# Expert up matrices in two transfers: the last three quarters go into the ring slot of the turn ahead

## What is computed

```python
def hier_moe(x, w_group, w_expert, w_gate, w_up, w_down):
    ...
    for e in range(N_EXPERTS):                                  # 32
        hid = jax.nn.silu(xf @ w_gate[e]) * (xf @ w_up[e])      # 1024 -> 512
        out = out + combine[:, e:e + 1] * (hid @ w_down[e])     # 512 -> 1024
```

## Time and profile before

| | us |
|---|---|
| median of three runs | 1307.29 |
| lowest and highest | 1305.0, 1307.72 |
| the profiled execution's own time | 1307.29 |
| its span, first to last instruction | 1305.5 |
| TensorE busy | 1045.1 (80%) |
| bytes read from HBM | 472.08 MB |

### The profile page before, as it was taken

The page is one execution under the profiler, slowest core; times in us unless marked ns, Lnnn a source line. Parts: engine busy times, 40 slices in busy tenths (PEclk is TensorE's granted clock), DMA queues, the critical chain, the costliest instruction groups (busy, mean ns, idle before and its releaser), DMA issues.

```text
span 1305.5 us, 26625 instructions
## 1 busy us (share of the span) xinstructions
PE 1045.1 (80%) x11057; PEld 641.9 (49%) x11057; DVE 483.5 (37%) x965; ACT 176.1 (13%) x413; POOL 108.7 (8%) x233
## 2 busy tenths in 40 slices
PE   9999989666766676679999999999675676756778
PEld 7885555333433333344688884555333333333333
DVE  2987534111111111136685888524121111211127
ACT  2343211000000000011111110211010000000011
POOL 0010111000010000000110110011000000000000
PEclk9999899888888888889999999998888888888889
DMA  9866999999999999999454237899999999999992
GB/s 362 303 268 266 358 426 424 428 431 426 429 430 427 429 430 426 430 411 387 146 188 159 102 133 313 333 426 426 427 428 429 428 428 429 429 427 430 428 419 100
DMA packets 59266, 473.87 MB, mean 363 GB/s; under 512 B 4328, under 2 KB 6632, under 8 KB 34000
## 3 DMA queue, kind: packets, MB, share of 16 engines
q1 hardware_dynamic: 57952, 469.73, 87.2%
q10 hardware_dynamic: 912, 2.12, 0.4%
q0 software_dynamic: 352, 1.32, 0.3%
HBM read 472.08 MB, written 3.16 MB: 364 GB/s over the span
## 4 chain that ended last, share of the span: by engine, by line
PE 47%; DMA 46%; issue 2%; DVE 2%; SPq 1%; ACT 0%; POOL 0%; DVEq 0%; POOLq 0%; ACTq 0%
DMA big<-in_moe_w_up_dram 43%; PE ps L1048 10%; PE ps L769 6%; PE ps L1267 6%; PE ps L1287 4%; PE ps L845 3%; PE ps L744 3%; PE ps L1179 3%; DMA big<-in_moe_w_down_dram 2%; PE ps L1073 2%; PE ps L725 1%; DMA big<-in_ple_w_gate_dram 1%; PE ps L735 1%; PE ps L1014 1%; PE ps L1081 1%
## 5 line engine op out<-in xcount | busy, mean ns | idle before, releaser
L1048 PE MATMUL ps<-big 128*32 128x256 f32 x4048 | 323.6, 487 | 236.5 <-DMA big<-in_moe_w_up_dram 232.6
L1048 PEld LDWEIGHTS ps<-big 128*32 128x32 f32 x4048 | 167.3, 139 | 391.3 <-issue 230.2
L1997 DVE SCALAR_TENSOR_TENSOR wroute<-wroute,ps 64x256 f32<-64x256 f32 x64 | 26.4, 413 | 649.2 <-ACT wroute L1521 649.2
L1073 PE MATMUL ps<-big,r 128*32 128x256 f32 x2048 | 122.8, 379 | 2.4 <-DVE r L2006 2.1
L1521 ACT ACTIVATE wroute<-ps 64x256 f32<-64x256 f32 x64 | 24.2, 378 | 546.8 <-PE ps L1048 546.8
L2509 POOL TENSOR_TENSOR big<-big,rk 128x64 f32<-128x64 f32 x64 | 28.4, 444 | 733.7 <-PE ps L1060 711.9
L1073 PEld LDWEIGHTS ps<-big,r 128*32 128x32 f32 x2048 | 64.5, 110 | 37.7 <-DVE r L2006 3.8
L1081 PE MATMUL ps<-big 32*128 32x256 f32 x1024 | 73.3, 400 | 1.3 <-ACT big L1532 1.3
L1014 PE MATMUL ps<-xn,big 128*32 128x256 f32 x1024 | 67.3, 380 | 1.6 <-POOL big L2503 1.6
L1081 PEld LDWEIGHTS ps<-big 32*128 32x128 f32 x1024 | 46.3, 184 | 29.1 <-issue 27.7
L1371 ACT ACTIVATE big<-ps 128x256 f32<-128x256 f32 (+3 forms) x58 | 25.5, 454 | 173.6 <-PE ps L1267 48.5
(11 more groups left out here) (296 smaller groups left out, 1202.0 us busy)
## 6 DMA issues: line engine op xcount, KB each, us to landing
big<-in_moe_w_gate_dram SPq DMA_DIRECT2D x62, 2048.0 KB, 32.9
big<-in_moe_w_down_dram SPq DMA_DIRECT2D x61, 2048.0 KB, 38.5
big<-in_moe_w_up_dram SPq DMA_DIRECT2D x60, 2048.0 KB, 37.1
big<-in_od_w_in_dram SPq DMA_DIRECT2D x12, 2048.0 KB, 14.1
big<-in_ev_w_in_dram SPq DMA_DIRECT2D x5, 2048.0 KB, 21.3
big<-in_ple_w_gate_dram SPq DMA_DIRECT2D x8, 1024.0 KB, 19.8
big<-in_od_w_out_dram SPq DMA_DIRECT2D x4, 2048.0 KB, 7.8
big<-in_ev_w_out_dram SPq DMA_DIRECT2D x2, 2048.0 KB, 14.0
```

Of the source, the lines that this page charges most:

```text
L1048: ins = nc.tensor.matmul(ps[TOK * i:TOK * i + TOK, 5, 0:2 * P].rearrange("p (b n) -> p b n", b=2), xe[:, k, :], here, start=k == 0, stop=k ...
L1073: ins = nc.tensor.matmul(ps[TOK * q:TOK * q + TOK, 7, 0:QD], hidT[:, k, :], wd[:, k, q * QD:(q + 1) * QD], start=k == 0, stop=k == KF - 1)
```

## The change

From expert 4 on, an up matrix is loaded in two transfers. Rows 0 and 1 of 8 (`LOW` = 2, 4 KB per partition) go into the expert's own up slot, turn e % 3. Rows 2 to 7 (12 KB per partition) go to the same rows of the up slot of turn (e - 1) % 3. The part that expert 3 leaves unused in its slot is where expert 4's high rows go; in general the high rows of expert e take the place of those of expert e - 3.

The order on SP becomes: gate 4 first and second half, **high rows of up 4**, down 3; then for experts 4 to 6: low rows of up e, gate e+1, high rows of up e+1, down e; in the hardware loop: low rows, high rows, down, gate of the next. For expert 31 the first piece (rows 0 to 3) becomes two (rows 0 and 1, rows 2 and 3).

The high rows count on the gate semaphore of their turn, so from expert 4 on TensorE waits there for two transfers of each expert, gate and high rows. `holder` frees the up slots accordingly: an up slot is now also held by the expert whose high rows lie in it.

```diff
--- before.py
+++ after.py
@@ -86,6 +86,7 @@
 
 AHEAD = (GATE, DEPTH)
 LENT = (UP, DEPTH)
+LOW = 2
 RELEASED_BY_HALVES = (0, DOWN, DEPTH - 1)
 IQ_PARTS = 0, HALF // 2, HALF, KD
 LAST_PARTS = (HALF, HALF + 2, KD), (KF // 2, KF - 1, KF)
@@ -103,7 +104,8 @@
 
     apart = DEPTH if kind == GATE else LAST
     twice = kind == GATE and ring_turn(GATE, EARLY) == j
-    return l * (sum(ring_turn(kind, e) == j for e in range(NE) if e != apart) + twice)
+    high = kind == GATE and sum(ring_turn(GATE, e) == j for e in range(EARLY, LAST))
+    return l * (sum(ring_turn(kind, e) == j for e in range(NE) if e != apart) + twice + high)
 
 
 ROTATED = ("rq0", "rq1", "rk0", "rk1")
@@ -573,12 +575,29 @@
                 dst = held(EXPERT_SLOTS[l][j][kind], *((KF, D) if kind == DOWN else (KD, BLK)))
                 sync.dma_start(dst.unsqueeze(1), w[:, ds(e, 1), :, :]).then_inc(weights_landed[j][kind], 16)
 
+            def expert_up_low(l, e, j):
+
+                sync.dma_start(held(EXPERT_SLOTS[l][j][UP], KD, BLK)[:, 0:LOW, :].unsqueeze(1),
+                               eu[l][:, ds(e, 1), 0:LOW, :]).then_inc(weights_landed[j][UP], 16)
+
+            def expert_up_high(l, e, j):
+
+                sync.dma_start(held(EXPERT_SLOTS[l][(j - 1) % DEPTH][UP], KD, BLK)[:, LOW:KD, :].unsqueeze(1),
+                               eu[l][:, ds(e, 1), LOW:KD, :]).then_inc(weights_landed[(j - 1) % DEPTH][GATE], 16)
+
             def last_parts(l, kind):
 
                 bounds = (0, *LAST_PARTS[kind - 1])
                 dst = held(EXPERT_SLOTS[l][LAST % DEPTH][kind], *((KF, D) if kind == DOWN else (KD, BLK)))
                 for i, landing in enumerate(part_landed[kind - 1]):
                     ks = slice(bounds[i], bounds[i + 1])
+                    if kind == UP:
+                        if i == 0:
+                            sync.dma_start(dst[:, 0:LOW, :], eu[l][:, LAST, 0:LOW, :]).then_inc(landing, 16)
+                            ks = slice(LOW, bounds[1])
+                        high = held(EXPERT_SLOTS[l][(LAST - 1) % DEPTH][UP], KD, BLK)
+                        sync.dma_start(high[:, ks, :], eu[l][:, LAST, ks, :]).then_inc(landing, 16)
+                        continue
                     sync.dma_start(dst[:, ks, :], (eg, eu, ed)[kind][l][:, LAST, ks, :]).then_inc(landing, 16)
 
             def slot_free_of(l, i):
@@ -663,13 +682,15 @@
                 sync.dma_start(place[:, 0:HALF, :], eg[l][:, EARLY, 0:HALF, :]).then_inc(begun, 16)
                 expert_read(l, GATE, 0)
                 sync.dma_start(place[:, HALF:KD, :], eg[l][:, EARLY, HALF:KD, :]).then_inc(begun, 16)
+                expert_up_high(l, EARLY, EARLY % DEPTH)
                 expert_read(l, DOWN, 0)
                 expert(l, DOWN, DEPTH, 0)
                 for e in range(EARLY, EARLY + DEPTH):
                     expert_read(l, UP, e - DEPTH)
-                    expert(l, UP, e, e % DEPTH)
+                    expert_up_low(l, e, e % DEPTH)
                     if e < EARLY + DEPTH - 1:
                         expert(l, GATE, e + 1, e % DEPTH)
+                        expert_up_high(l, e + 1, (e + 1) % DEPTH)
                     expert_read(l, DOWN, e - DEPTH)
                     expert(l, DOWN, e, e % DEPTH)
                 expert_read(l, GATE, EARLY)
@@ -677,9 +698,11 @@
                 with sync.Fori(1, (LAST - EARLY) // DEPTH) as it:
                     for j in range(DEPTH):
                         e = it * DEPTH + EARLY + j
-                        for kind in (UP, DOWN):
-                            expert_read(l, kind, it * DEPTH + EARLY - DEPTH + j)
-                            expert(l, kind, e, (EARLY + j) % DEPTH)
+                        expert_read(l, UP, it * DEPTH + EARLY - DEPTH + j)
+                        expert_up_low(l, e, (EARLY + j) % DEPTH)
+                        expert_up_high(l, e, (EARLY + j) % DEPTH)
+                        expert_read(l, DOWN, it * DEPTH + EARLY - DEPTH + j)
+                        expert(l, DOWN, e, (EARLY + j) % DEPTH)
                         expert_read(l, GATE, it * DEPTH + EARLY - DEPTH + 1 + j)
                         expert(l, GATE, it * DEPTH + EARLY + 1 + j, (EARLY + j) % DEPTH)
                 for kind in (UP, DOWN):
@@ -688,6 +711,8 @@
                 for e in range(NE - DEPTH, NE):
                     for kind in range(3):
                         holder[EXPERT_SLOTS[l][ring_turn(kind, e)][kind]] = expert_read, l, kind, e
+                        if kind == UP and e > NE - DEPTH:
+                            holder[EXPERT_SLOTS[l][(e - 1) % DEPTH][UP]] = expert_read, l, UP, e
             for name, _ in loads.plain[2]:
                 plain(name)
 
@@ -1025,6 +1050,8 @@
                     elif e is not None:
                         n = n if kind != GATE or e < DEPTH else (e - 1) // DEPTH
                         j = ring_turn(kind, e)
+                    if kind == GATE and (e is None or e >= EARLY):
+                        n = n * 2 - (e == LAST)
                     if kind == GATE and j == ring_turn(GATE, EARLY) and e != j:
                         n = n + 1
                     if kind == GATE or e != LAST:
@@ -1036,14 +1063,17 @@
                     w = [weights(kind, n, j, e).rearrange("p k (b h n) -> p k h b n", b=2, h=2)
                          for kind, n in ((GATE, nn[0]), (UP, nn[1]))]
                     high = w
+                    if e is None or e == LAST:
+                        rows = held(EXPERT_SLOTS[l][(j - 1) % DEPTH][UP], KD, BLK).rearrange("p k (b h n) -> p k h b n", b=2, h=2)
+                        high = [rows[:, LOW:HALF], rows[:, HALF:KD]]
                     if e == LENT[1]:
                         pe.wait_ge(lent_landed, 32 * (l + 1))
                         high = [rows.rearrange("p k (b h n) -> p k h b n", b=2, h=2) for rows in (between, lent)]
                     for k in range(KD):
                         if e == LAST and k in (0, *LAST_PARTS[0]):
-                            pe.wait_ge(part_landed[0][sum(b <= k for b in LAST_PARTS[0])], 16 * (l + 1))
+                            pe.wait_ge(part_landed[0][sum(b <= k for b in LAST_PARTS[0])], (16 + 16 * (k == 0)) * (l + 1))
                         for i in range(4):
-                            up = (w[1][:, k] if high is w or k < 2 else high[0][:, k - 2] if k < HALF else high[1][:, k - HALF])
+                            up = (w[1][:, k] if high is w or k < LOW else high[0][:, k - LOW] if k < HALF else high[1][:, k - HALF])
                             here = w[0][:, k, i % 2] if i < 2 else up[:, i % 2]
                             ins = nc.tensor.matmul(ps[TOK * i:TOK * i + TOK, 5, 0:2 * P].rearrange("p (b n) -> p b n", b=2),
                                                    xe[:, k, :], here, start=k == 0, stop=k == KD - 1)
```

## The result

| kernel | us, median | runs |
|---|---|---|
| before | 1307.05 (1305.0 to 1309.39) | 11 |
| changed | 1311.97 (1309.13 to 1313.02) | 11 |

The ratio is 1.0036, with a 95% interval of 1.0028 to 1.0043: the change makes the kernel 3.7 to 5.6 us slower, where 4.4 had been forecast. The profiled executions have spans of 1305.5 and 1310.2 us. In the experiments, each kernel stands beside runs of the kernel before on its own chip. A ratio leaves out executions more than 1.5% over the fastest of the same kernel, which concerns three of the six of part_halves.

What follows compares the result with a forecast made beforehand. The DMA engines' time for their rows was taken to bound both expert stages. 56 cuts at 0.080 us (4.5) less 0.1 for the early issue took 1307.3 to 1311.7 us, 1309.5 to 1314 with bounds and scatter; wider range 1307.0 to 1315.5.

Steps and rivals of the forecast that it cites:

- The bound: Both mixture-of-experts stages: their length is the time the DMA engines need for their rows, share 1.01 at 427 GB/s.
- The early issue: Before the loop: 1.5 MiB of up 4 issued ahead of down 3; gain 0.1 us, bounds 0 and 0.2.
- Who is put back: Down 3, 4 and 5 land up to 3.7 us later, embedding's gate issues at about 563.2 us; cost 0.
- SP held up inside the loop: Stalls of 2.6 to 7.1 us per SP issue at stage end may occur in the loop; DMA engines lose nothing.
- The cost of a cut: Up matrices in both stages: 0.080 us more per cut, bounds 0.067 to 0.10; 56 cuts, 4.5 us.
- The sum: Whole kernel: 4.5 - 0.1 = 4.4 us slower, 1307.3 + 4.4 = 1311.7 us; forecast's chance 0.68.
- The free cut: Rival, up matrices: slow windows have other causes, 56 cuts cost under 2.6 us, say 1308.5 us; chance 0.20.
- the used lead: Rival, between gate 4's second half and the loop: earlier bytes save up to 3.7 us a layer, 1304.4 us; chance 0.05.
- a second cutting of the 12 KB rows: Rival, high parts of up matrices: cut again, for instance into 8 and 4 KB, fixed part paid twice, 1316.2 us; chance 0.05.
- a latency paid in series: Rival, each of 56 additional transfers: pays its 1.5 us latency one after another, 1391 us; chance 0.02.

Runs made afterwards that it cites:

- part_halves: Like cut_only, but each up matrix of experts 4 to 30 split into partitions 0 to 63 and 64 to 127, rows whole at 16 KB; ratio 1.4709.
- after_again: The changed kernel run once more, beside no_lead_again on the same chip; 1311.42 us, ratio 1.0049 to the kernel before.
- no_lead_again: Changed kernel, but expert 4's high rows go out only after expert 1's product, with its low rows; run beside after_again: 1311.43 us, ratio 1.0039.
- cut_only: Changed kernel's 4 and 12 KB cut, but both parts in the expert's own slot at the old place, no early issue; 1312.17 us, ratio 1.0052.
- cut_half: Like cut_only, but the up matrix is cut in the middle into two parts with 8 KB rows; 1312.41 us, ratio 1.0049.
- three: Changed kernel, but the high rows of experts 4 to 30 come in two transfers of 6 KB rows; 1315.98 us, ratio 1.0077.
- part_odd: Like part_halves, but the two transfers take the even and the odd partitions, rows whole at 16 KB; 1308.08 us, ratio 1.0013.
- rows2: Like cut_half, but one transfer brings the even 2 KB rows and the other the odd ones, eight pieces per partition; 1335.34 us, ratio 1.0226.

## Why the prediction was right, point by point

**The bound.** The stages are as long as the DMA engines need for their rows. TensorE's busy time in the loop, the share of 1.01 and the waits for up matrices are as before, and the time from expert to expert grows with the rows alone.

**The early issue.** The row was to stand 0.4 us behind gate 4's second half; SP's issues of after:

```profile
154.72 0.33 SPq L684 DMA_DIRECT2D big<-in_moe_w_gate_dram  x1
155.09 0.89 SPq L585 DMA_DIRECT2D big<-in_moe_w_up_dram  x1
158.95 0.33 SPq L576 DMA_DIRECT2D big<-in_moe_w_down_dram  x1
```

So the change does what it says. The gain was put at 0.1 us, between 0 and 0.2. The medians of after_again and no_lead_again differ by 0.01 us, and each ratio has an interval of some 1.6 us to either side: the large lead of that rival, 3.7 us a layer, is excluded, the 0.1 is not resolved. The DMA rate between 156 and 230 us was named as the sign of a lead that is used: it is 421 GB/s before and 422 after, so it does not rise visibly. Beside the cut kernels without a lead, the windows above point to more than 0.2 us in layer 0. If that holds, this term was too small, and so was the cost of the change without its lead; the two misses would offset each other in the sum.

**Who is put back.** Down 4 answers to the earlier trace rows: issued at 166.64 us, it now takes 19.6 us to land instead of 16.7, and TensorE begins with it at 203.41.

```profile
DMA to landing us min/median/max: 19.6/19.6/19.6
```

```profile
203.41 1.93 PE L1103 MATMUL ps<-big,r 128*32 128x256 f32 x32 [0.48 <-DVE r L2036]
```

It lands at 186.2 and has 17 us to spare. At the end of layer 0 the first half of the embedding's gate goes out at 562.53 us, for which 563.2 had been said:

```profile
562.53 13.32 SPq L566 DMA_DIRECT2D big<-in_ple_w_gate_dram  x4
```

The DMA rate from 560 to 577 us is 411 GB/s at a share of 1.00 (before 413): the queue was not empty, and the later release cost nothing that shows.

```profile
560.00:577.00 17.00, 13.70 (x220) 8.06 (x212) 3.61 (x10) 1.83 (x5) 0.50 (x1) 0.89 1.00 411
```

**SP held up inside the loop.** It was said that SP may meet a full queue in the loop too, without harm. It does. SP's issue times of after for the high rows and for down matrices (ns, least, median, most):

```profile
L585 SPq DMA_DIRECT2D big<-in_moe_w_up_dram x54: 332/2120/3691, 155.1 to 1217.6; - x54
L576 SPq DMA_DIRECT2D big<-in_moe_w_down_dram x61: 327/3597/3916, 89.9 to 1220.7; - x61
```

Before, the median for a down matrix was 333 ns:

```profile
L574 SPq DMA_DIRECT2D big<-in_moe_w_down_dram x61: 327/333/470, 90.0 to 1216.4; - x61
```

The engines lose nothing by it: the share stays at 1.01. Nor do SP's stalls set the pace in the changed kernel. From 160 to 530 us SP still waits 152.3 us for gate and up products (232.2 before):

```profile
SPq L576 <- PE ps L1078: 152.3, 24, 14.1
```

**The cost of a cut.** The term of the sum was 0.080 us, from a line through two rates of the kernel before, with bounds of 0.067 and 0.10. The loops of five kernels give 0.066 to 0.085, about 0.075 in the middle. The line had used rows of the embedding's gate and of the odd layer's projections; the rival that these are slow for other reasons (0.20) falls with cut_only, cut_half and three, whose rows are all of expert matrices.

That 0.080 came so close is in part luck. The window that stood for rows of 4 KB (1262 to 1272 us) is mixed. The DMA view of the kernel before, for that window alone, gives:

```profile
DMA packets 958, 4.09 MB, mean 409 GB/s; under 512 B 83, under 2 KB 83, under 8 KB 837
```

So 837 - 83 = 754 rows of 4 KB bring 3.09 MB, and the other quarter of the bytes came in longer rows (nearly all of 8 KB in the packet records). Counted so, this window gives an estimate of 0.10 for a set of rows, not 0.080. The test on expert 31 is mixed too: its window holds 778 - 95 = 683 rows of 4 KB, of which expert 31 has only 512. The window with 2 KB rows holds one row length: from it and the 16 KB rows the line has a slope of (4.888 - 0.679) / 14 = 0.3006 and a fixed part of 0.078, closest to what was measured.

**The sum.** 4.5 - 0.1 = 4.4 us were forecast, 4.9 lie between the medians, 4.7 between the two spans. By the time from expert to expert, 28 x (0.085 + 0.066) = 4.2 us come from the cuts. From expert 0's product to expert 31's, the stages of the changed kernel are 2.0 and 1.0 us longer than before, those of after_again 2.5 and 1.9, where 2.2 each had been said (for the last landing). The stage between the layers, from expert 31's product to expert 0's of layer 1, takes 274.89 us before, 277.60 in the profiled execution of the changed kernel and 274.89 again in after_again; so the 2.7 us that it adds in the first pair are scatter. Expert 0's product comes 1.5 us earlier in that execution, which is scatter too. So it is partly luck that the two spans differ by as much as 4.7 us.

The chances add up a little differently from what is said: 0.68 less a tenth, with the second cut and the series, is 0.68 and not 0.70.

**The rivals.** The free cut, the used lead (3.7 us a layer, 1304.4 us), a second cutting of the 12 KB rows (the packets rose by exactly one set a cut) and a latency paid in series (part_odd) are all excluded. The page of the Trainium skill, "DMA: Bandwidth & Descriptors", whose Specifications give 512 B as the least transfer for line rate, is not borne out here if that is read for rows in a full queue: 429, 424 and 414 GB/s stand beside one another in loops that differ in the rows of one matrix in three. The 2.0 us that the prediction takes from its "Anatomy of one DMA" are given there for transfers issued from GpSimd, while SP issues those of this kernel; in part_odd 54 more of these add nothing to the time of the loop.

No run points to a kernel that beats the one before: in its loop every row already has the whole 16 KB that a matrix gives a partition.

## What to carry to other kernels

Where windows show the DMA engines full from end to end, moving a transfer earlier is worth little (here at most about 1 us of 1312), and the price of a layout is the number of rows into which it cuts the bytes: about 0.075 us for 128 rows here, paid at every expert. Such a price can be read before it is paid, from two stretches of the old profile that differ in row length and are both full; each should hold rows of one length only. And where a cost is paid at every turn of a loop, the time from turn to turn prices it to about a hundredth of a us, while whole executions scatter by several. Ask first whether the queue was ever empty after the moment at which the earlier issue becomes possible.

## What the runs showed that was not expected

Transfers over 64 neighbouring partitions are slow: with one matrix in three split this way the loop fell from 429 to 249 GB/s. With 2.097 MB each for gate, up and down, an expert takes 6.29 MB / 249 GB/s = 25.3 us instead of 14.7. If gate and down kept their 4.9 us each, the split matrix would take 15.5 us, three times as long as before. But gate and down seem to be slowed too: in the trace's packet records from 300 to 500 us the median row of 16 KB takes 1.17 us instead of 0.61, so more rows are slow than the third that belongs to up matrices. The same split into even and odd partitions leaves the rate at 428. Why is not shown.

SP's stalls go with the rows, not with the number of transfers. In part_odd, with as many transfers as cut_half but whole rows, the median issue of a down matrix takes 341 ns, in cut_half 2,973; in rows2, again with as many transfers, it takes 10,134. The views are the issue times by line of part_odd and then of cut_half:

```profile
L576 SPq DMA_DIRECT2D big<-in_moe_w_down_dram x61: 327/341/469, 89.9 to 1217.4; - x61
```

```profile
L576 SPq DMA_DIRECT2D big<-in_moe_w_down_dram x61: 327/2973/3643, 89.6 to 1220.3; - x61
```
